# Two layers with two attentions on one core: probabilities folded into one square before their transposes, and work of the last attention moved between engines

## The reference, cut to what matters

```
# first attention, per group: distance 0..128 in the strided sequence
band = (rel >= 0) & (rel <= steps)            # steps = 128
m = max(logits); p = exp(logits - m); s = sum(p)
num = p @ v                                   # unnormalised; groups are merged later
# last attention: distance 0..127, with a sink in the denominator
in_window = (dist >= 0) & (dist < WINDOW)     # WINDOW = 128
p = exp(logits - m); denom = sum(p) + exp(sink - m)
o = (p @ v) / denom;  y = o * silu(z)
```

## Time and profile before

| | |
|---|---|
| median of 3 runs | 2566.18 us (2565.63 to 2566.23) |
| the profiled execution | 2566.36 us, of which its span is 2564.6 us |
| busy share of the span | PE 97%, DVE 55%, POOL 44%, ACT 40% |
| chain that ended last | PE 79%, DVE 13%, ACT 5% |
| first attention's slots with quads | about 181.6 to 608.1 us |
| last attention's slots | about 2206.9 to 2471.1 us |

### The profile page before, as it was taken

One profiled execution on the slowest core, in us unless ns is written; L12 is line 12 of the kernel. 1 busy time (PEld: TensorE's weight loads), 2 busy tenths in 40 slices (PEclk: granted clock), 3 DMA queues, 4 the chain that ended last, 5 costly groups with the idle time before them and its releaser, 6 DMA issues.

```text
span 2564.6 us, 41617 instructions
## 1 busy us (share of the span) xinstructions
PE 2497.5 (97%) x15824; PEld 2015.9 (79%) x15824; DVE 1398.5 (55%) x2664; ACT 1019.0 (40%) x1992; POOL 1130.0 (44%) x1390
## 2 busy tenths in 40 slices
PE   7999999999999999999999999999999999999999
PEld 6887777777777777777788878788888888777777
DVE  3002253345866657576632677766666007588843
ACT  4125646556433333242113453555554115344421
POOL 3332222223433243231457545677776554545452
PEclk9999999999999999999999999999999999999999
DMA  4241211211201111011432332333334115101132
GB/s 141 84 131 46 62 55 58 72 56 42 66 23 53 35 34 51 26 59 63 165 127 73 105 103 98 108 99 101 107 106 172 42 56 154 45 26 30 30 114 84
DMA packets 234438, 198.94 MB, mean 78 GB/s; under 512 B 7296, under 2 KB 202240, under 8 KB 233728
## 3 DMA queue, kind: packets, MB, share of 16 engines
q1 hardware_dynamic: 188800, 120.60, 15.6%
q10 hardware_dynamic: 45440, 75.68, 8.3%
HBM read 150.64 MB, written 45.61 MB: 77 GB/s over the span
## 4 chain that ended last, share of the span: by engine, by line
PE 79%; DVE 13%; ACT 5%; issue 2%; POOL 1%; DMA 0%; ACTq 0%; DVEq 0%; SPq 0%; POOLq 0%
PE gemm L808 13%; PE gemm L810 13%; PE gemm L809 13%; PE gemm L1269 5%; PE gemm L1271 5%; PE gemm L1270 5%; PE scores L880 2%; PE weighted L908 1%; PE probs_t L893 1%; DVE neg_logits L2318 1%; PE weighted L1496 1%; PE scores L1347 1%; PE probs_t L1140 1%; DVE prob L2331 1%; DVE prob L2330 1%
## 5 line engine op out<-in xcount | busy, mean ns | idle before, releaser
L758 POOL CAST w_hi<-w_raw 128x512 fp32r<-128x512 f32 x264 | 188.3, 713 | 1182.6 <-PE gemm L810 1039.6
L760 POOL TENSOR_TENSOR w_lo<-w_raw,w_hi 128x256 fp32r<-128x256 f32 x528 | 441.9, 837 | 41.7
L808 PE MATMUL gemm<-h_hi,w_hi 128*128 128x512 f32 x1072 | 449.0, 419 | 1.2 <-DVE h_lo L1964 1.2
L810 PE MATMUL gemm<-h_hi,w_lo 128*128 128x512 f32 x1072 | 420.2, 392 | 0.0
L809 PE MATMUL gemm<-h_lo,w_hi 128*128 128x512 f32 x1072 | 418.9, 391 | 0.0
L1617 DVE CUSTOM_DVE_ANT_0 neg_logits<-scores,bias_tile 128x128 f32<-128x128 f32 (+1 forms) x192 | 67.7, 352 | 339.6 <-PE scores L880 334.4
L808 PEld LDWEIGHTS gemm<-h_hi,w_hi 128*128 128x128 f32 x1072 | 202.1, 189 | 48.1 <-issue 14.2
L810 PEld LDWEIGHTS gemm<-h_hi,w_lo 128*128 128x128 f32 x1072 | 201.2, 188 | 44.2
L809 PEld LDWEIGHTS gemm<-h_lo,w_hi 128*128 128x128 f32 x1072 | 202.4, 189 | 32.7 <-issue 1.7
L808 PE MATMUL gemm<-xn_hi,w_hi 128*128 128x512 f32 x288 | 117.7, 409 | 1.9 <-DVE xn_lo L2235 1.7
L3152 ACT ACTIVATE prob<-neg_logits,stats 128x256 f32<-128x256 f32 (+1 forms) x128 | 63.5, 496 | 135.2 <-DVE stats L2318 132.1
(11 more groups left out here) (639 smaller groups left out, 6126.5 us busy)
## 6 DMA issues: line engine op xcount, KB each, us to landing
w_raw<-in_w_in SPq DMA_DIRECT2D x73, 512.0 KB, 3.9
w_raw<-in_a_w_in SPq DMA_DIRECT2D x28, 512.0 KB, 4.0
w_raw_b<-in_a_w_in SPq DMA_DIRECT2D x20, 512.0 KB, 4.7
gates_scratch<-o_f ACTq DMA_DIRECT2D x32, 256.0 KB, 2.0
merge_gates<-gates_scratch ACTq DMA_DIRECT2D x4, 2048.0 KB, 10.2
mlp_v_scratch<-v_piece ACTq DMA_DIRECT2D x32, 256.0 KB, 2.0
mlp_v<-mlp_v_scratch ACTq DMA_DIRECT2D x16, 512.0 KB, 4.1
w_raw<-in_a_w_out SPq DMA_DIRECT2D x16, 512.0 KB, 4.1
```

The source lines that it names most:

```text
L758: Q(pool.tensor_copy(weight_part(u, 0, ks), raw[:, s, ks, :]))
L760: Q(pool.tensor_tensor(weight_part(u, 1, ks), raw[:, s, ks, :], weight_part(u, 0, ks).bitcast(F32), ALU.subtract), E("w_split") if ks.stop ...
L808: pe.matmul(dst, w_high, hi(k, h), start=first, stop=False)
L810: m = pe.matmul(dst, w_low, hi(k, h), start=False, stop=last)
```

## The change

1. **First attention, one more slot of lag.** Transposes move from s-1 to s-2 and `weighted`, with `collect`, from s-2 to s-3. `prob` gets a second buffer for the quads before number 44. Quads 45 to 47 use one buffer: their `exps` wait for the transposes of the quad before, which are now a slot later.
2. **First attention, fold in 20 of 48 quads**: groups 0 and 1 of pair 0 (8 quads), and of the other pairs the quads 0, 1, 6 and 7. DVE `fold` (three operations) saves the diagonal of the previous block in `same_key`, adds the previous block onto the own one and subtracts the diagonal. PE transposes four blocks. DVE `parted` (three operations) replaces ACT's `copy_back`: one mask, the diagonal added again, the other mask.
3. **Last attention, regrouped.** The multiplication by the reciprocal becomes four ACT operations of 128x128 (`normalised2` on ACT, first in ACT's slot, for c-1). `gated2` moves to ACT too. What is left on DVE, `folded2` (denominator, reciprocal, add), is now for quad c itself and stands last in DVE's slot, behind the wait for that quad's `exps2`.

```diff
-        prob = at("prob", 168, [P, 4, 256])
+        prob = [at(f"prob{n}", kb, [P, 4, 256]) for n, kb in enumerate((168, 102))]
+        same_key, later_keys = at("same_key", 144, [P, 4, P]), at("later_keys1", 146, [P, P])
...
+        LAST_G2 = 12 * PAIRS - 4
+        def prob_of(c):
+            return prob[c % 2 if c < LAST_G2 else 0]
+        def probs_free(c):
+            return c if c > LAST_G2 else c - 1
+        def folds(c):
+            p, g, t = quads[c]
+            return g < 2 and (p == 0 or not 2 <= 4 * g + t <= 5)
...
             def transposes(c):
+                if folds(c):
+                    pe.wait_ge(E("probs_folded"), folded_to(c))
                 for i, hh, ti in quad:
-                    for b in key_blocks(g, 2 * t + ti):
+                    for b in (1,) if folds(c) else key_blocks(g, 2 * t + ti):
...
-                if s - 1 in slot_of:
-                    transposes(slot_of[s - 1])
                 if s - 2 in slot_of:
-                    weighted(slot_of[s - 2])
+                    transposes(slot_of[s - 2])
+                if s - 3 in slot_of:
+                    weighted(slot_of[s - 3])
...
+            def fold(c):
...
+                dve.wait_ge(E("exp_done"), c + 1)
+                same = same_key[:, prev, :]
+                V(v.tensor_tensor(same, before, ident.unsqueeze(1).to_broadcast([P, same.shape[1], P]), ALU.mult))
+                V(v.tensor_tensor(own[:, prev], own[:, prev], before, ALU.add))
+                V(v.tensor_tensor(own[:, prev], own[:, prev], same, ALU.subtract), E("probs_folded"))
+            def parted(c):
+                dve.wait_ge(E("pt_full"), c + 1)
+                if c > 0:
+                    dve.wait_ge(E("pv_full"), c)
...
+                V(v.tensor_tensor(before, both[:, prev], later_keys[:].unsqueeze(1).to_broadcast([P, same.shape[1], P]), ALU.mult))
+                V(v.tensor_tensor(before, before, same, ALU.add))
+                V(v.tensor_tensor(ptsb[:, :, P:256], both, causal.unsqueeze(1).to_broadcast([P, 4, P]), ALU.mult), (E("pt_done"), c + 1))
...
             for s in range(A_END):
+                if s - 2 in slot_of and folds(slot_of[s - 2]):
+                    parted(slot_of[s - 2])
                 if s in slot_of:
                     biased(slot_of[s])
-                if s - 2 in slot_of:
-                    collect(slot_of[s - 2])
+                if s - 3 in slot_of:
+                    collect(slot_of[s - 3])
+                if s - 1 in slot_of and folds(slot_of[s - 1]):
+                    fold(slot_of[s - 1])
...
-            def normalised2(c):
+            def folded2(c):
                 dve.wait_ge(E("exp_done"), len(quads) + c + 1)
...
-                V(v.tensor_tensor(own[:, with_prev], own[:, with_prev], prev[:, with_prev], ALU.add))
-                V(v.tensor_tensor(own, own, den.unsqueeze(2).to_broadcast([P, 4, P]), ALU.mult), E("pn_done"))
+                V(v.tensor_tensor(own[:, with_prev], own[:, with_prev], prev[:, with_prev], ALU.add), E("w_rows"))
...
-                if 0 <= c - 1 < 4 * QP:
-                    normalised2(c - 1)
...
-                if 0 <= c - 3 < 4 * QP:
-                    gated2(c - 3)
...
+                if 0 <= c < 4 * QP:
+                    folded2(c)
...
             def exps(c):
-                if c > 0:
-                    act.wait_ge(E("pt_full"), c)
+                if c > 1:
+                    act.wait_ge(E("pt_full"), probs_free(c))
...
-                if s - 1 in slot_of:
-                    copy_back(slot_of[s - 1])
+                if s - 2 in slot_of and not folds(slot_of[s - 2]):
+                    copy_back(slot_of[s - 2])
...
+            def normalised2(c):
+                act.wait_ge(E("w_rows"), PAIRS + c + 1)
+                for x in range(4):
+                    own = pr2[:, c % 2, x, P:256]
+                    A(a.activation(own, own, ACT.Copy, scale=den2[:, c % 2, x:x + 1]), (E("probs_folded"), FOLDS + c + 1) if x == 3 else None)
+            def gated2(c):
+                act.wait_ge(E("pv_full"), len(quads) + c + 1)
+                A(a.activation(ys[:, i, 256 * t:256 * t + 256], PV[:, 0:256], ACT.Copy), (E("pv_free"), len(quads) + c + 1))
...
             for s in range(S_SLOTS + 1):
                 c = s - 3
+                if 0 <= c - 1 < 4 * QP:
+                    normalised2(c - 1)
+                if 0 <= c - 3 < 4 * QP:
+                    gated2(c - 3)
                 if 0 <= c < 4 * QP:
                     exps2(c)
```

More of the change, by code:

```diff
@@ L475, in build, with folded_to @@
         A_END = A_SLOTS + 8
+        LAST_G2 = 12 * PAIRS - 4
[6 more added lines that the diff above has]
+            return g < 2 and (p == 0 or not 2 <= 4 * g + t <= 5)
+        def folded_to(c):
+            return sum(folds(i) for i in range(c + 1))
+        FOLDS = folded_to(len(quads) - 1)
         LAST = PAIRS - 1
@@ L1630, in collect, with prev_tiles @@
                 V(v.tensor_copy(natural(numer[p % 2][:, g:g + 1, :], g, t), permuted(PV[:, 0:256].unsqueeze(1), g)), E("pv_free"))
+            def prev_tiles(g, t):
+                return slice(0, 4) if g == 0 and t else slice(1, 4, 2)
+            def fold(c):
+                p, g, t = quads[c]
+                prev = prev_tiles(g, t)
+                own, before = prob_of(c)[:, :, P:256], prob_of(c)[:, prev, 0:P]
+                if c == 0:
+                    for n in (6, 7):
+                        dve.wait_ge(E(f"load_{n}"), 64)
+                    dve.wait_ge(E("c_in_bs_in"), 32)
+                    V(v.tensor_scalar(later_keys[:], causal, -1.0, 1.0, ALU.mult, ALU.add))
+                dve.wait_ge(E("exp_done"), c + 1)
[4 more added lines that the diff above has]
+            def parted(c):
+                p, g, t = quads[c]
+                prev = prev_tiles(g, t)
+                dve.wait_ge(E("pt_full"), c + 1)
+                if c > 0:
+                    dve.wait_ge(E("pv_full"), c)
+                both = PT2[:].rearrange("p (n k) -> p n k", n=4)[:, :, P:256]
+                before, same = ptsb[:, prev, 0:P], same_key[:, prev, :]
+                V(v.tensor_tensor(before, both[:, prev], later_keys[:].unsqueeze(1).to_broadcast([P, same.shape[1], P]), ALU.mult))
+                V(v.tensor_tensor(before, before, same, ALU.add))
+                V(v.tensor_tensor(ptsb[:, :, P:256], both, causal.unsqueeze(1).to_broadcast([P, 4, P]), ALU.mult), (E("pt_done"), c + 1))
             def best_of(p):
@@ L2341, in parted2 @@
                 V(v.tensor_tensor(pts2[:, :, P:256], both, causal.unsqueeze(1).to_broadcast([P, 4, P]), ALU.mult))
[L2342 to L2348, removed]
+                V(v.tensor_tensor(pts2[:, with_prev, 0:P], both[:, with_prev], later[:].unsqueeze(1).to_broadcast([P, n_prev, P]), ALU.mult), (E("pt_done"), len(quads) + c + 1))
             def gate2(i):
+                dve.wait_ge(E("pv_free"), len(quads) + 4 * i + 4)
                 V(v.scalar_tensor_tensor(ys[:, i, :], ys[:, i, :], 0.5, zs2[:, i % 2, :], ALU.mult, ALU.mult), E("gated"))
@@ L2476, in copy_back @@
                 for j, (sl, b0) in enumerate(todo):
-                    A(a.activation(ptsb[:, sl, b0 * P:256], src[:, sl, b0 * P:256], ACT.Copy), E("pt_done") if j == len(todo) - 1 else None)
+                    A(a.activation(ptsb[:, sl, b0 * P:256], src[:, sl, b0 * P:256], ACT.Copy), (E("pt_done"), c + 1) if j == len(todo) - 1 else None)
             def exps(c):
```

11 lines of the change are left out of this document (7 added, 4 removed).

## The result

| | before | after |
|---|---|---|
| median | 2566.10 us (10 runs, 2564.92 to 2567.48) | 2571.78 us (10 runs, 2570.81 to 2574.32) |
| profiled execution, its span | 2566.36, 2564.6 | 2574.32, 2572.5 |

What follows compares the result with a forecast made beforehand. The prediction took PE to bound the first attention and a loop through DVE and ACT, set by DVE's queue order, the last. -3.6 (first) and +4.9 (last) sum to +1.3 us: 2567.5 us, range 2556 to 2576.

Steps and rivals of the forecast that it cites:

- The loop in the last attention: Last attention: DVE and ACT work one after the other each quad, 8.05 us a quad against 7.72 before.
- Its size, +4.9: Last attention: its end comes 4.9 us later through the slower DVE and ACT sequence; bounds 0 and +12.4.
- ACT's multiplication, 0.33 us each: Last attention: four ACT multiplications by the reciprocal take 0.33 us each, 1.3 together; upper bound 0.40 each.
- `scores2` will hold PE: Last attention: PE's waits for DVE move to `scores2`; for quad 31 it waits until 2449.0, against 2445.71 before.
- Free work in DVE's 2 us of waiting: Last attention: z, gate and q, at most 3 us a slot, fit into DVE's 3.3 us wait for ACT, costing nothing.
- First attention, -3.6: First attention: -5.7 for 52 fewer transposes, +1.4 fold stalls, -1.2 at pairs' starts, +1.9 at the end: -3.6 us.
- The lag and the end: First attention: the extra slot gives -1.2 us at the pairs' starts and +1.9 at the last statistics, together +0.7.
- The term of the end: First attention's last statistics: single-buffered quad 47's later exponentials cost +1.3, with one more `copy_back` +1.9 us.
- The fold with its stalls: First attention: 52 fewer transposes save 5.7 us, and PE waiting for DVE's `fold` in pair 0 costs 1.4.
- Rival A: Last attention: DVE and ACT fit under PE's pace, all 14.35 us of waits go, 2548.2 us; chance 0.10.
- Rival B: Last attention: POOL draws out the fold's adds, up to +12.4 us, 2577 us; chance 0.30 shared with other slower outcomes.
- Rival C: Last attention keeps its old pace, only the first attention counts, 2562 us; included in the 0.48 for the forecast.

Runs made afterwards that it cites:

- copy_on_dve: The changed kernel with `gated2`, the copy out of PSUM, back on DVE behind `biased2` and z: 2573.84 us, ratio to the kernel before 1.0029.
- fold_next_slot: The changed kernel with `folded2(c)` moved into the next slot, between `parted2(c-1)` and `biased2(c+1)`: 2545.30 us, ratio to the kernel before 0.9921.
- unwaited_parted: The changed kernel, but `parted2` raises its semaphore without a value, as in the kernel before: 2568.45 us, ratio to the kernel before 1.0011.
- order_only: The kernel before, work on its old engines, DVE's last-attention order now `parted2(c-2)`, `gated2(c-3)`, `normalised2(c-1)`, `biased2(c)`, z and q: 2568.36 us, ratio 1.0010.
- fold_all: The changed kernel with `folded2` in the next slot and the first attention's fold in all 32 quads of groups 0 and 1: 2573.25 us, ratio 1.0029.
- last_only: The kernel before with the last attention's change alone: 2573.66 us, ratio to the kernel before 1.0032.

## Why the prediction was right or wrong, point by point

- **What bounds the kernel:** right. PE in the first attention, the order of DVE's queue in the last one.
- **The loop in the last attention:** the mechanism was right, and shown by three edits: 0.12 us less in the loop gave 3.3 us, one multiplication more cost 25.6 (0.83 a quad), and taking `parted2` out of it, which put it below PE's own pace, gave 26. The last is not only the loop's own excess: in the new order PE's waits of the kernel before go as well.
- **Its size, +4.9:** the failed term. In the profiled execution the stage was 11.7 us longer. To the 4.9 come: 0.12 x 30 = 3.5 because `parted2` now waits for its own end (I took 1.33 us "until the next `biased2` starts" from a row of the kernel before, whose wait the diff changes); 1.2 of small pieces (0.7 each in the step to the exponentials and at the alibi tiles, a pair of which took 1.28 instead of 0.62 at the quads 8 and 20, 0.4 before the add, less 0.3 at the add and 0.2 in the first step, which took 6.47 where the forecast has 6.72); 0.7 at the end, where ACT's multiplications are longer and behind other operations; 1.45 of half clock, in that execution. Sum 11.75. By medians the last attention cost less than that trace says: 8.1 alone, and 9.6 as the whole less the first part. The prediction had named "an uncounted 0.15 us a quad" as a way to be slower; it did not see which.
- **ACT's multiplication, 0.33 us each:** 0.403 measured, the upper bound. The Trainium skill's budget ("ScalarE: Activation LUTs", Rules for kernel authors), 0.3 us and 0.83 ns an element, gives 0.41, an estimate that the row bears out: it was better than my subtraction of rows. It mattered only at the end of the stage.
- **"`scores2` will hold PE":** half right. PE waits 5.3 us there, and 13.0 at the transposes. Where a slower loop shows up in PE's list depends on which of its products PE asks for first.
- **Free work in DVE's 2 us of waiting:** right for the pace (copy_on_dve, 8.14 against 8.13 us a quad); the medians leave up to 2 us open.
- **First attention, -3.6:** -3.9 measured, and part of the closeness is luck. The lag and the end were +0.7 and measured +0.8. The term of the end has a slip: 0.44 + 2.1 - 1.0 is 1.5, not 1.3. The fold with its stalls was -5.7 + 1.4 = -4.3, and -5.0 came. PE's wait for `fold` was over-sized: 1.4 predicted, 0.2 in the trace, which leaves 5.2 for the 52 transposes.
- **Rival A** (all waits go, 2548.2) did not happen in this kernel. It did where the loop is below PE's pace (fold_next_slot, 2545.3), and gave a little more than its price.
- **Rival B** (adds drawn out by POOL): not as the bound it was. The wide adds took 845 ns on average, 874 before, none above 1.11 us. The rule in the Trainium skill ("SBUF — State Buffer", Who interferes with whom) would let an add wait a whole POOL operation, and the prediction read the mean of 874 ns against it, as partial loss. That reading was wrong. The mean is low because 10 of the 24 wide adds of the kernel before meet no POOL operation; the 14 that meet one wait for its end, as the page says. The prediction also left out that the small addition of the sink waits too, up to 0.71 us.
- **Rival C** (old pace): no, 8.13 against 7.72 us.

## What to carry to other kernels

Before counting what an engine is relieved of, follow one work unit round all engines and write down the loop that its queue order closes; here, with the same work on the same engines, the place of `folded2`'s three operations in one queue decided between 5.7 us slower and 20.2 us faster than before. In that loop every wait counts once per unit, also an engine's wait for itself: when a diff changes the form of a signal, read what is waited for. The list of PE's waits names the last releaser, not the pace. An engine that waits at every single unit is where to start looking, but no proof: in the kernel before, ACT waited for `biased2` at all 32 quads, and the loop through it did not set the pace there.

```profile
ACT prob L3152 <- DVE stats L2318: 132.1, 32, 17.9
```

Only the sum of one unit round, beside the pace of the bounding engine, tells.

## What the runs showed of the hardware

- From the start of a DVE operation (128x512, 0.69 us) to the start of the next it is 0.73 us when DVE waits for the first one's end, and 0.61 us when it doesn't (22 places each, after and unwaited_parted). The Trainium skill ("VectorE: DVE Perf Modes", The DRAIN you can't avoid) reports eight copies in a row that took the same time with a semaphore after each and with one after the last. Here, behind a read from PSUM and before an independent operation, the wait cost 0.12 us, and for this pair the measurement decides. The same section adds that a next operation that is not held starts earlier, with which the 0.61 agrees.
- An addition of two SBUF operands on DVE that starts during a POOL operation (a two-input one or a cast of the weights) waits for its end: 128x4 ends 0.02 us after it instead of taking 0.16, 128x512 ends 0.55 after it instead of taking 0.69 (11 and 12 cases in after; the kernel before has the same, 12 and 14). The POOL operation that starts during a drawn-out add is longer too, 0.94 instead of 0.61 us at quad 15.
- PE's clock fell to 1.2 GHz for 3.4 us after a wait of 1.80 us (after) and one of 2.63 us (order_only), and for 6.8 us from within each of three waits of 6.0 us (fold_all). It stayed at 2.4 GHz after waits of 1.69 us (unwaited_parted) and 1.84 us (last_only) at the same place, and after three of 1.80 us in fold_all. So the length of the last wait alone does not decide it; what else does stays open.
